# A three-block transformer kernel on one core: low parts of the context half of two norms computed by GpSimd instead of VectorE

## The reference

```python
def _rms(x, g):
    x32 = x.astype(jnp.float32)
    y = x32 * lax.rsqrt(jnp.mean(x32 * x32, axis=-1, keepdims=True) + EPS)
    return (y * g.astype(jnp.float32)).astype(x.dtype)
...
        x = x + g1 * o
        h = _rms(x, norm2_g[i]) * (1.0 + sc2) + sh2
        x = x + g2 * _swiglu(h, ffn_w_gate[i], ffn_w_up[i], ffn_w_down[i])
        if not last:
            y = y + cg1 * oc
            hc = _rms(y, norm2_g[i]) * (1.0 + csc2) + csh2
            y = y + cg2 * _swiglu(hc, ffn_w_gate[i], ffn_w_up[i], ffn_w_down[i])
```

## Time and profile before

| | |
|---|---|
| median of 3 runs | 2321.68 us (2320.24 to 2327.1) |
| profiled execution | 2324.39 us |
| its span, first to last instruction | 2322.6 us |
| PE busy | 94% |
| DVE busy | 59% |
| ACT busy | 39% |
| POOL busy | 7% |
| chain that ended last: PE / DVE / ACT | 80% / 12% / 3% |

### The profile page before, as it was taken

One profiled execution on the slowest core, in us unless ns is written; L12 is line 12 of the kernel. 1 busy time (PEld: TensorE's weight loads), 2 busy tenths in 40 slices (PEclk: granted clock), 3 DMA queues, 4 the chain that ended last, 5 costly groups with the idle time before them and its releaser, 6 DMA issues.

```text
span 2322.6 us, 36304 instructions
## 1 busy us (share of the span) xinstructions
PE 2193.8 (94%) x13050; PEld 1828.7 (79%) x13050; DVE 1381.2 (59%) x2472; ACT 894.4 (39%) x1399; POOL 160.1 (7%) x249
## 2 busy tenths in 40 slices
PE   6999899999989999999999899987899999999998
PEld 3654488887876658999997578876789999999997
DVE  4544344342269563664777443989766666666666
ACT  3234322222243363434476101128544444444444
POOL 0021000000013030000000000018200000000000
PEclk8999999999989999999999999999999999999999
DMA  8265232322252274555543233430355555555553
GB/s 310 105 217 187 73 104 95 99 95 95 92 146 84 100 245 137 183 179 182 199 148 107 78 126 119 144 120 0 101 189 190 181 190 189 181 190 189 181 190 127
DMA packets 92838, 340.62 MB, mean 147 GB/s; under 512 B 10409, under 2 KB 10436, under 8 KB 92496
## 3 DMA queue, kind: packets, MB, share of 16 engines
q1 hardware_dynamic: 89280, 325.10, 41.3%
q0 software_dynamic: 3472, 14.35, 2.1%
HBM read 338.36 MB, written 1.05 MB: 146 GB/s over the span
## 4 chain that ended last, share of the span: by engine, by line
PE 80%; DVE 12%; ACT 3%; issue 2%; DMA 1%; DVEq 0%; POOL 0%; ACTq 0%; SPq 0%; POOLq 0%
PE bank L768 19%; PE bank L1042 15%; PE bank L1030 13%; PE bank L535 11%; PE bank L795 8%; PE bank L897 3%; DVE main_zone L1498 2%; DVE main_zone L1615 2%; DVE tail_zone L1495 1%; DVE first_w_parts L1501 1%; PE bank L574 1%; DVE main_zone L1501 1%; PE bank L740 1%; PE bank L719 1%; PE bank L728 1%
## 5 line engine op out<-in xcount | busy, mean ns | idle before, releaser
L768 PE MATMUL bank<-act_parts,first_w_parts 128*128 128x512 f32 (+1 forms) x2928 | 559.9, 352 | 20.3 <-DVE act_parts L1498 13.0
L768 PEld LDWEIGHTS bank<-act_parts,first_w_parts 128*128 128x128 f32 x2928 | 475.4, 193 | 101.3 <-issue 19.7
L1042 PE MATMUL bank<-w_parts,a_parts 128*128 128x512 f32 x1536 | 370.5, 392 | 4.4 <-DVE a_parts L1501 3.4
L1501 DVE TENSOR_TENSOR first_w_parts<-weight_ring,first_w_parts 128x1024 fp32r<-128x1024 f32 x166 | 211.6, 1276 | 259.8 <-ACT first_w_parts L1189 259.6
L1501 DVE TENSOR_TENSOR w_parts<-weight_ring,w_parts 128x1024 fp32r<-128x1024 f32 x235 | 286.8, 1221 | 90.5 <-ACT w_parts L1189 90.5
L1042 PEld LDWEIGHTS bank<-w_parts,a_parts 128*128 128x128 f32 x1536 | 282.6, 189 | 59.5 <-issue 5.1
L1030 PEld LDWEIGHTS bank<-n_parts,w_parts 128*128 128x128 f32 x2568 | 322.1, 191 | 8.3
L1189 ACT ACTIVATE w_parts<-weight_ring 128x1024 fp32r<-128x1024 f32 x235 | 248.0, 1056 | 199.4 <-PE bank L1030 159.0
L1030 PE MATMUL bank<-n_parts,w_parts 128*128 128x256 f32 x2568 | 324.6, 283 | 0.0
L1189 ACT ACTIVATE first_w_parts<-weight_ring 128x1024 fp32r<-128x1024 f32 x166 | 175.0, 1056 | 226.4 <-PE bank L768 126.8
L535 PE MATMUL bank<-main_zone,weight_ring 128*128 128x256 f32 (+1 forms) x976 | 242.7, 410 | 1.5 <-DVE main_zone L1674 0.8
(11 more groups left out here) (226 smaller groups left out, 1981.6 us busy)
## 6 DMA issues: line engine op xcount, KB each, us to landing
weight_ring<-in_stream SPq DMA_DIRECT2D x618, 512.0 KB, 3.4
main_zone<-in_rel_bias POOLq DMA_DIRECT2D x6, 512.0 KB, 14.4
main_zone<-in_decay POOLq DMA_DIRECT2D x1, 1536.0 KB, 8.7
main_zone<-in_xT POOLq DMA_DIRECT2D x1, 1024.0 KB, 11.5
main_zone<-in_ctxT POOLq DMA_DIRECT2D x1, 1024.0 KB, 16.0
tail_zone<-in_rel_bias POOLq DMA_DIRECT2D x2, 512.0 KB, 26.6
tail_zone<-in_keysT POOLq DMA_DIRECT2D x1, 1024.0 KB, 5.0
out<-main_zone SPq DMA_DIRECT2D x2, 512.0 KB, 2.6
```

What stands on the lines that cost most here:

```text
L768: mm = pe.matmul(o[:, 0:w], wb[:, hw, k, :], fin[:, hx, k, 0:w], start=(k == 0 and n == 0), stop=(k == DC - 1 and n == 2))
L1042: mm = pe.matmul(acc[n][:, :], ap_[:, e % 3, ha, (n // 2) * P:(n // 2 + 1) * P], wp[(B + b) % PARTS][:, hw, (n % 2) * 512:(n % 2 + 1) * 51 ...
L1501: return dve.tensor_tensor(o, a, b, op)
```

## The change

In the two norms DVE makes the low part of the latent half only. The context half of each chunk's low part is made by POOL in two instructions: `raw + shift`, written over `raw` (a tensor_scalar of 128x256), then, behind a wait on POOL's own semaphore `ctx_shifted`, minus the high part (a tensor_tensor of 128x256). POOL starts a chunk when ACT's high part of it is there. PE now waits for two semaphores ahead of each chunk's matmuls in the first tile behind these norms, `normed` and `normed_ctx`, behind `norm(2)` too, where the first tile reads only latent columns. 16 DVE instructions go, 32 POOL instructions come.

```diff
+        normed_ctx = sem("context_normed")
+        ctx_shifted = sem("context_shifted")
...
                     if j == 0:
                         pe.wait_ge(normed, DC * k_norm + k + 1)
+                        if k_norm in (1, 2):
+                            pe.wait_ge(normed_ctx, DC * (k_norm - 1) + k + 1)
...
-                    for a, b, s in halves(n):
+                    for a, b, s in halves(n)[:1 if k in (1, 2) else 2]:
                         last = stt(fin[:, 1, c, a:b], raw[:, c, a:b], shift(c, s),
                                    fin[:, 0, c, a:b].bitcast(F32), ALU.add, ALU.subtract)
                     last.then_inc(normed, 1)
...
             attention(0)
 
+            def context_low(k):
+
+                d = norms[k]
+                for c in range(DC):
+                    pool.wait_ge(fin_hi, DC * k + c + 1)
+                    shift = MOD[:, d["layer"], 24 * d["which"] + c, 1:2]
+                    x = raw[:, c, L:T]
+                    pool.tensor_scalar(x, x, shift, 1.0, ALU.add, ALU.mult).then_inc(ctx_shifted, 1)
+                    pool.wait_ge(ctx_shifted, DC * (k - 1) + c + 1)
+                    pool.tensor_tensor(fin[:, 1, c, L:T], x, fin[:, 0, c, L:T].bitcast(F32), ALU.subtract).then_inc(normed_ctx, 1)
+
+            context_low(1)
+            context_low(2)
             evacuated(pool, "ffn_d0", DC)
             pool.wait_ge(normed, DC * 3)
```

## The result

| | before | with the change |
|---|---|---|
| median, 20 runs each | 2324.48 us | 2329.80 us |
| lowest to highest | 2316.5 to 2329.58 | 2322.93 to 2337.66 |
| ratio, 95% interval | | 1.0027 [1.0017, 1.0037] |
| span of the profiled execution | 2322.6 us | 2323.8 us |

The interval says 3.9 to 8.6 us more, its middle is 6.3 us, and the medians lie 5.3 us apart. The two profiled spans differ by 1.2 us only; why that can't be read as the change's price stands further down. So the prices are read in the two norms.

A forecast was written before the change was run, and what follows sets the result against it. DVE was taken to bound both norms at 1.58 us a chunk. Pace and block, 2 x (1.6 + 0.7) = +4.6 us, gave 2329.0 us from the profiled execution, 2326.3 by the median; range 2319 to 2333.

The forecast's parts named there:

- Removal: In each norm, eight DVE low halves go; seven can shorten the path, saving at most 2.8 us a norm, 5.5 in both.
- POOL's prices: Per chunk in the norms, POOL's tensor_scalar takes 0.48 us, its own wait 0.13 and its tensor_tensor 0.80.
- The estimate of 0.61: Alternative price in us of POOL's 256-column tensor_tensor in the norms; it would lower the forecast by 3.0 us; not used.
- Bare sum: POOL's two operations and own wait per norm chunk without turns, 1.41 us, against DVE's 1.58 before.
- Turns: In the norms DVE's low parts and POOL's operations, inputs in SBUF, alternate; POOL's period grows by 0.21 to 1.62 us.
- that rival: In the norms DVE's scalings are held up by POOL as well: +9.3 us in each, 2340 us; chance 0.03.
- The weight block's turn: Behind DVE's last low half, the next weight block's low part pushes POOL's last chunk back by 0.94: +0.7 us a norm.
- +1.6 us a norm: POOL's period of 1.62 us over eight chunks lets PE go on in norm(1) at 289.56 instead of 288.00.
- The clock: Rival: gaps in PE's work in norm(1) keep the clock low behind it: +1.9 us, 2328.2 us; chance 0.17.
- A sign that misled: At the norm's end: the forecast is wrong if PE's last wait ends before 288 in the trace.
- PE's second wait: PE's added wait ahead of eight matmuls of the first tile, in the same place as the first, costs nothing.
- POOL keeps up: Rival: in the norms POOL's period is 1.41 to 1.2 us, giving about 2320 us, at best 2316.2; chance 0.20.

The follow-up runs named there:

- no context low parts: The change with the context low parts of both norms not made and not waited for; norms 10.54 and 10.53 us, before 13.29, one execution.
- one column: The change with DVE's latent low parts in both norms cut to one column of 256; each norm 13.11 us, before 13.29, one execution.
- late wait: The change with PE's wait for POOL's context parts of norm(2) moved from tile 0 to tile 8; ratio 0.9999 against the kernel before.
- block waits: The change with DVE waiting for POOL's last chunk before making the next weight block's low part; ratio 1.0014 against the kernel before.
- norm(1) only: The change in norm(1), the code of before in norm(2); ratio 1.0012 against the kernel before.
- spread context: Kernel before plus one POOL operation a chunk in norm(1); norm(2) latent halves first, context work spread behind, low parts by POOL; ratio 0.9975.
- Latents first: Kernel before, without POOL work, norm(2) making all latent halves first and context halves behind, PE waiting for those in tile 8; ratio 0.9983.

## Why the prediction was right, and where its steps were not

The forecast was +4.6 us and no change that can be told (0.79); measured were 3.9 to 8.6 us more, middle +6.3, 0.27%. "Under 0.3%" came true, but the forecast also held that such a difference can't be told from none, and with 20 runs each the interval excludes no difference. The median of 2329.80 us lies in the range; the kernel before took 2324.48 in these runs and 2321.68 in those shown first, so 2.8 of the 3.5 us between forecast and result are not the change's.

- **Removal.** Eight low halves a norm went; the bound of 2.8 us for it was 2.75 (no context low parts).
- **POOL's prices.** tensor_scalar 0.48: measured 0.478 alone. Own wait 0.13: 0.07. tensor_tensor 0.80 from the line through two large ones: 0.73. Bare sum 1.28, not 1.41. The estimate of 0.61 worked out from the Trainium skill (GPSIMD Engine Reference, section 3.1, Elementwise) is 0.12 too low, the line through the two rows 0.07 too high; here the measurement decides.
- **Turns.** Right in kind: low halves 0.73 in place of 0.48, scalings unchanged (that rival is out). The growth of POOL's period was put on the tensor_tensor with 0.21; it fell on the tensor_scalar with 0.16 to 0.17. So the pace was 1.44 in place of 1.62.
- **The weight block's turn.** Foretold as +0.7 a norm; it cost 0.98 above a tensor_scalar without a turn, 0.82 above one with the usual turn. In "one column" it fell on the tensor_tensor, so the operation that is hit is not fixed.
- **The norm's price.** The step that was mis-sized is "+1.6 us a norm" for the pace. Pace and block together were put at 2.3 and measured 1.47 and 1.52; of the 1.47 the block is 0.82, which leaves 0.65 for the pace. From ACT's first high part to PE (274.17 to 287.10) the trace of the change adds up as 0.08 + tensor_scalars 0.78 + 6 x 0.64 + 1.46 + own waits 8 x 0.07 + tensor_tensors 7 x 0.73 + 0.95 + 0.14 = 12.92 of 12.93 us; before, that stretch took 11.47 (276.53 to 288.00). Without any turn it would be 0.08 + 8 x (0.48 + 0.07 + 0.73) + 0.14 = 10.46. By this estimate turns cost 2.5 us and the bare work gained 1.0: the difference is the loss.
- **The clock.** The rival had it late in norm(1). It was not: a granted clock of 1.00 was there at 280. It came late behind norm(2) (+1.33 us), which I had left at its old time; with that the place was wrong and the size (1.9) near. Whether it comes late there in most executions is open. This and the smaller norm price cancel: 1.47 + 2.85 = 4.3 against 2 x 2.3 = 4.6. The total was right partly by that luck.
- **A sign that misled.** That PE's last wait of the norm ends before 288 was named as a sign of being wrong, and it came true (287.10), but only because norm(1) started 2.37 us earlier in this execution, at 272.34. From the first scaling the wait ends at 14.76 us, before at 13.29: the sign had to be a length, not a time in the trace.
- **PE's second wait** was costed at nothing because it stands in the same place as the first. That missed that behind norm(2) it binds PE to POOL too early: moved to tile 8, 3.1 us come back (late wait).
- **"POOL keeps up"** was the only rival with a gain (0.20). In two operations it doesn't; with one a chunk it does.

**What stays open.** The yardstick explains 4.3 of 6.3 us; the interval begins at 3.9, so nothing need be missing. But in "block waits" and "norm(1) only" too the middle of the interval lies above the sum, by 2.2 and 1.3 us, so a cost outside these stretches is not ruled out. The spans of the two profiles differ by only 1.2 us because they differ where no changed code runs: norm(1) itself starts at 272.34 in place of 274.71 (in the twelve profiles at 270.29 to 277.04, with the same code ahead of it), and a mask addition fell on other DVE operations near 700 us (of the 2.8 us by which the change is behind at 694, counted from norm(2)'s first scaling, 1.3 are left at 712.80, before 711.25), both in favour of the change; against it stands 1.6 us at the boundary of `gate_up` and the down projection (last section). Why these fall as they do was not tried.

## What to carry to other kernels

Ask not only what an operation costs on GpSimd, but which DVE operations with all inputs in SBUF stand beside it, and above all which long one DVE has ready when GpSimd comes to its last piece. Here one operation per chunk on GpSimd and the second on an engine that doesn't take turns with it (ACT) made 11.56 us a norm in place of 14.76. And put the wait for a result where it is first read: norm(2) with its two tiles then took 17.69 us with the same work on GpSimd, before 17.98.

## What the runs showed of the hardware that was not expected

- PE starts 0.14 us behind POOL's end, and 0.04 us behind DVE's; POOL's wait on its own semaphore takes 0.07 us.
- A POOL operation that waits for its turn is recorded as long, not as idle (1.46 us for a tensor_scalar of 0.48), and DVE's next operation (the block at 284.58) got its turn ahead of POOL's next one, though POOL's stood back to back.
- PE stands still between `gate_up` and the down projection in both kernels (in the windows below this lies in 522 to 525). The pause is 2.31 us in all twelve profiles. In nine of them the granted clock falls to 0.50 (1.2 GHz) behind it; before, in "one column" and in "spread context" it stays at 1.00. "Latents first" is among the nine, and up to there its code is that of the kernel before: the change does not make the clock fall. Two stretches of the kernel with the change, and the same two before:

```profile
524.00:526.00 2.00, 1.71 (x6) 1.39 (x7) 0.26 (x2) 1.06 (x1) 0.00 (x0) 0.79 0.00 0
526.00:528.00 2.00, 2.00 (x6) 1.53 (x5) 1.20 (x1) 0.00 (x0) 0.00 (x0) 0.50 0.00 0
```
```profile
524.00:526.00 2.00, 0.79 (x3) 0.67 (x4) 1.05 (x2) 0.20 (x1) 0.00 (x0) 1.00 0.00 0
526.00:528.00 2.00, 2.00 (x10) 1.64 (x9) 1.11 (x1) 0.86 (x1) 0.00 (x0) 1.00 0.00 0
```

  Six matmuls in place of ten in the same 2 us. The second weight block's high part behind it (ACT, L1189 before and L1193 now) starts at 531.98 in place of 531.29, where the first had started 0.92 us earlier than before: 1.6 us in one profiled execution, at code that the change doesn't touch, and as large as what the change costs a norm. Why the clock falls there in some executions and not in others is open. A difference of spans between two single profiles can't price a change of this size; stretches around the changed code come nearer, and the runs side by side decide.
